# One more slab of the first projection computed among the modulation tiles, and the mixer tasks behind it dealt out anew

## The chip, the cores and the metric

The kernel runs on one core of a Trainium2 chip. The metric is device time in microseconds (us) for one execution; lower is better. Everything is float32, or float32 in the form that TensorE reads as fp32r.

## What is computed

The reference is a stack of four transformer-like layers over 256 tokens of width 2048. The part that matters here is the beginning of the first layer:

```python
c_act = jax.nn.silu(c)
mod = c_act @ w_ada[l] + b_ada[l]                       # 6 pieces of 2048
shift_a, scale_a, gate_a, shift_m, scale_m, gate_m = split(mod, 6)
h = rms_norm(x, g_pre_mix[l]) * (1.0 + scale_a) + shift_a
y = token_mixer(h, w_in[l], ...)                        # projection, conv, mLSTM, attention, w_out
x = x + gate_a * rms_norm(y, g_post_mix[l])
```

`token_mixer` multiplies h with `w_in` (2048 x 4616) and feeds the parts to a causal convolution, to an mLSTM with four heads and to a sliding-window attention with 16 heads.

## The kernel before

**Slabs.** Every weight matrix is cut into slabs of 2048 x 128 (1 MB, 16 blocks of 128 x 128). A slab gives 128 output features for all 256 tokens. The sequence of all slabs is numbered through the whole kernel; `w_in` of layer 0 has slabs 0 to 36, and `SLABS` says what each is: 0 `ka`, 1 `gate`, 2 `va`, 3 `qa0`, 4 `q0`, 5 `k0`, 6 `qa1`, 7 `v0`, 8 `v1`, 9 `qa2`, 10 `q1`, 11 `k1`, 12 `qa3`, and so on.

**An ordinary slab** takes three engines. It lands in one of five raw buffers (`RAW`, `RING` = 5). ScalarE copies it to `WH` in fp32r (`high`), VectorE subtracts that from the raw slab and writes the remainder `WL` (`low`), and TensorE (`slab`) multiplies 32 times with WH (the high and the low half of h, `HX`) and 16 times with WL. There are two places for WH and WL, taken in turn.

**The ramp.** The modulation is computed on VectorE: 16 tiles of `w_ada` for each of 12 pieces, each tile 1 MB, one `scalar_tensor_tensor` with a row sum (`tile`). The first two pieces, scale and shift, 32 tiles, have to be there before h is. They come in pairs, and after certain pairs (`RAMP_STEPS`) VectorE finishes the elements of scale and shift that are there (`ended`), forms x * scale * rms for those blocks of h (`scaled`, into `HF`), and ScalarE adds the shift. The first `RAMP` = 8 slabs of `w_in` are not split: they are loaded among the tiles (`RAMP_AT` gives the place in the order of loads, `RAMPW` the buffers) and multiplied in plain float32 with HF, block by block, as h comes (`ramp`). Each of the eight has a PSUM bank of its own (`BANK_OF`). `h_chunk_low` makes the low half of HX, four blocks at a time; three of the four chunks are made between tiles.

**Behind the ramp** each engine walks the slabs n = 8 to 36 of layer 0 in program order. At each slab ScalarE takes the result of slab n-1 out of PSUM, makes WH of slab n+1 and then does its mixer tasks; VectorE convolves if slab n-1 was q or k, computes the tiles that stand behind slab n (`AFTER`: further pieces of the modulation), makes WL of slab n+1 and then does its mixer tasks; TensorE multiplies slab n and then does its mixer tasks. Slabs 18, 21, 24, 27 and 30 are again computed in plain float32 from the raw buffer (`unsplit`). A mixer task i is whatever belongs behind slab i: `scores`, `turned` and `values` of an attention group, `m_scores`, `m_values`, `m_sum` of an mLSTM head, `gates`. In layer 0 the tasks 0 to 17 lag behind, because eight slabs were computed at once: `tasks_at` deals them to slabs 8 to 17 by hand.

**Waits that matter.** TensorE's `m_scores` of head 0, in task 8, waits for `s_grl`, which VectorE raises after it has split the gate rows `GRR`. VectorE's `attsums` in a task waits for ScalarE's `att_exp`, and that for VectorE's `att_max`. `m_divisor` waits through ScalarE for TensorE's `m_values`. All loads stand in one queue on SyncE: a load into a raw buffer waits until the load five places before it has been used up (`s_free`). Line 436 is the helper for all products, 440 for transposes, 949 for all of ScalarE's work; 1649 and 1657 are VectorE's `tensor_tensor` and `scalar_tensor_tensor`, 2648 a load into a raw buffer, 2699 a load of a ramp slab.

Of the kernel before, what the change touches and what calls it, by code (L numbers as in the profile page):

```python
# [13 lines left out]
T = 256  # L14
KT = 16
# [30 lines left out]

def tasks_at(l, n):

    late = {8: range(5), 9: (5,), 10: (6, 7), 11: (8,), 12: (9,), 13: (10, 11), 14: (12,), 15: (13, 14), 16: (15,),
            17: (16, 17)}  # L50
    return (n,) if l or n > 17 else late.get(n, ())


N_IN, N_LAYER = 37, 37 + 16 + 128
# [23 lines left out]

XN_AT = {2: 1, 3: 2, 4: 5, 5: 6}

RAMP = 8
RAMP_AT = [2, 6, 9, 13, 17, 21, 24, 28]
WIDE = {0, 1, 2, 5, 6, 7, 10, 11, 12}
RAMP_STEPS = [slice(_a, _b) for _a, _b in zip((0, 4, 8, 10, 12, 13, 14, 15), (4, 8, 10, 12, 13, 14, 15, 16))]


def spread(first, last, n):
# [1 line left out]

AFTER = ([9, 10, 11, 12, 13, 14, 15, 15, 16, 16, 17, 18, 19, 19, 20, 21, 22, 22, 23, 24, 25, 25, 26, 27, 28, 29, 30, 31,
          31, 32, 33, 33, 34, 35] + list(range(37, 51)) + spread(J_MLP[0] + 4, J_MLP[0] + 110, 82)
         + [J_IN[1] + n for n in (6, 7, 10, 15, 16, 18, 19, 24, 25, 29, 30, 31, 32, 33)]
         + [J_MLP[1] + n for n in (4, 6, 8)] + spread(J_MLP[1] + 19, J_MLP[1] + 31, 13))
# [54 lines left out]
    FREE_AT.append(_n)  # L150


BANK_OF = [j if 3 <= j < RAMP else (j + RAMP * (j < 3)) % 3 for j in range(N_SLABS)]

HI_AT, _n = [], 0
for _j in range(N_SLABS):
# [20 lines left out]

def before(j, of):

    return max([i for i in range(max(0, j - 8), j) if of[i] == of[j]], default=-1)  # L180


class Tally:
# [12 lines left out]
def build(nc, d, out):  # L196
    ctx = ExitStack()
    with ctx:
# [45 lines left out]
        CTANH = at("ctanh", (D,), A0)  # L244
        RAMPW = [m(f"rampw{r}", (KT, 128), off) for r, off in enumerate((12, 20, 28, 0, 52, 60, 68))]
        RAMPW.append(at("rampw7", (KT, 128), WL_AT + 8 * kb * PLACE_OF[RAMP + 1]))
        HF = m("hf", (KT, T), 36)
        SQ = m("sq", (KT, T + 1), 60)
        SQT = SQ[:, :, 0:T]
# [109 lines left out]
        s_a, s_v = sem("s_a"), sem("s_v")  # L359
        s_one, s_c, s_ct0, s_cb0 = sem("s_one"), sem("s_c"), sem("s_ct0"), sem("s_cb0")  # L360
        s_crow = sem("s_crow")
        s_rampw = [sem(f"s_rampw{r}") for r in range(RAMP)]
        s_hf = sem("s_hf")
        s_xs, s_xsum, s_rx = sem("s_xs"), sem("s_xsum"), sem("s_rx")
        s_ysq, s_yg, s_y2 = sem("s_ysq"), sem("s_yg"), sem("s_y2")
# [60 lines left out]
        def tensor(e):  # L426
# [58 lines left out]
            def ramp():  # L485


                banks = [claim(BANK_OF[r]) for r in range(RAMP)]

                def part(r, k):  # L490
                    return mm(banks[r][:, 0:T], RAMPW[r][:, k, :], HF[:, k, :], k == 0, k == KT - 1)

                here = []
                for q in RAMP_STEPS:
                    for r in range(len(here), RAMP):
                        if RAMP_AT[r] < 2 * q.stop:
                            here.append(r)
                            e.wait_ge(s_rampw[r], 16)
                            for k in range(q.start):
                                part(r, k)  # L500
                    for r in here:
                        for k in range(q.start, q.stop):
                            e.wait_ge(s_hf, k + 1)
                            last = part(r, k)
                        if q.stop == KT:
                            last.then_inc(s_slab, 1)
                for r in range(3, RAMP):
                    release[r] = (s_ev, r + 1)

            def side(i):  # L510

# [155 lines left out]
            def mixer_after(l, n):  # L667
                for i in range(8):
                    a = AT_SLAB["qa", i]
                    if n == a + 6:  # L670
                        turned(l, i)
                    if n == a + 7:
                        values(l, i)
                    if n == a + 1:
                        scores(l, i)
                if n == AT_SLAB["qa", 7] + 9:
                    att_sum(l)
                for i, s in enumerate(SLABS):
                    if s in V_ORDER and n == i + 1:
                        v_turned(l, i, TV[V_ORDER[s] % 2])  # L680
                if n == AT_G + 5:
                    gates(l)
                for h in range(4):
                    if n == AT_S[h]:
                        m_scores(l, h)
                    if n == AT_V[h]:
                        m_values(l, h)
                    if n == AT_V[h] + 2:
                        m_sum(l, h)
# [255 lines left out]
        def scalar(e):  # L945
# [24 lines left out]

            def whole(j):

                e.wait_ge(s_slab, j + 1)
                if j - 1 not in BY_SCALAR:
                    e.wait_ge(s_ev, j)
                return BK[BANK_OF[j]][:, 0:T]

            def log_and_exp():

# [12 lines left out]
                act(SX[:, :], BK[3][:, 0:T], ACT.Copy)  # L992
                rsqrt(RS[:, :], BK[3][:, 0:T], D, LN0[:, :], s_rx)

            def to_h_first(c, shift):

                q = slice(4 * c, 4 * c + 4)
                for k in range(4 * c, 4 * c + 4):
                    e.wait_ge(s_hs, k + 1)
                    act(HF[:, k, :], HF[:, k, :], ACT.Identity, bias=shift[:, k:k + 1]).then_inc(s_hf, 1)  # L1000
                e.wait_ge(s_hf, 4 * c + 4)
                act(HX[:, q, 0, :], HF[:, q, :], ACT.Copy).then_inc(s_hh, 1)

# [369 lines left out]
            def layer(l):  # L1373
                for n in range(0 if l else RAMP, N_IN):
                    if l == 0 and n == RAMP:
                        for i in range(RAMP):
                            mixer_half(l, i)
                    elif n:
                        mixer_half(l, n - 1)
                    for i in tasks_at(l, n):  # L1380
                        mixer_first(l, i)
                    if l or n != N_IN - 1:
                        next_high(J_IN[l] + n)
                    if l == 0 and n == N_IN - 2:
                        next_high(J_IN[l] + N_IN - 1)
                    if l and n == N_IN - 1:
                        out_gate(l, 5)
                    for i in tasks_at(l, n):
                        mixer_tasks(l, i)
                gate = modulation(l, GATE_A)  # L1390
                for n in range(16):
                    if n == 0:
# [235 lines left out]
            x_rms_first()  # L1628
            e.wait_ge(s_prm, 16)
            for c in range(4):  # L1630
                to_h_first(c, MOD[:, SHIFT_A, :])
            high(RAMP)
            layer(0)
            to_h(1, modulation(1, SHIFT_A))
# [5 lines left out]
        def vector(e):  # L1640
# [88 lines left out]
                e.wait_ge(s_mod, PIECES.index((l, piece)) - 1)  # L1729
                return MOD[:, 6 * l + piece, :]  # L1730

            def scaled(k, gs, first=False):
                stt((HF if first else SQT)[:, k, :], X[:, k, :], gs[:, k:k + 1], RS[:, :], ALU.mult,
                    ALU.mult).then_inc(s_hs, 1)

            def h_chunk_low(i, c):
# [309 lines left out]
            def mixer_tasks(l, n):  # L2046
                if n == AT_G + 4:
                    gates_scanned(l)
                if n == AT_G + 6:
                    e.wait_ge(s_gt, l + 1)  # L2050
                    e.tensor_copy(AC[:, :, :], BK[5][:, 0:8].rearrange("p (a h) -> p a h", a=2)).then_inc(s_ac, 1)
                    e.wait_ge(s_grh, l + 1)
                    tt(GRR[32:36, :, :], GR[0:4, :, :], GRR[0:4, :, :].bitcast(F32), ALU.subtract).then_inc(s_grl, 1)
# [540 lines left out]
                q = slice(512 * b, 512 * b + 512)  # L2594
                stt(CB[:, q], CTANH[:, q], 1.0, BK[4 + b][:, :], ALU.add, ALU.mult).then_inc(s_cb0, 1)
            e.wait_ge(s_cb0, 4)
            gs, sh = MOD[:, SCALE_A, :], MOD[:, SHIFT_A, :]
            for k in range(KT):
                tile(k)
                tile(16 + k)  # L2600
                if k % 4 == 0 and k:
                    h_chunk_low(-1, k // 4 - 1)
                for q in RAMP_STEPS:
                    if k == q.stop - 1:
                        e.wait_ge(s_prm, 16)
                        e.wait_ge(s_free, FREE_AT[TILE_POS[16 + k]])
                        ended(0, q)
                        settled(ended(1, q))
                        if k == 3:
                            e.wait_ge(s_rx, 1)  # L2610
                        for i in range(q.start, q.stop):
                            scaled(i, gs, True)
            for l in range(2):
                s0 = PER_LAYER * l + SINK
                settled(ts(MINUS_SINKS[:, 16 * l:16 * l + 16], PRM[:, s0:s0 + 16], -1.0, None, ALU.mult))
# [21 lines left out]
        def sync(e):  # L2637
# [56 lines left out]
            for place, (kind, n) in enumerate(LOADS):  # L2694
                if place in RAMP_AT:
                    r = RAMP_AT.index(place)
                    if r == 3:
                        e.wait_ge(s_crow, 4)
                    e.dma_start(RAMPW[r][:, :, :].rearrange("p a b -> p (a b)"), source(r)).then_inc(s_rampw[r], 16)
                if kind == "slab":  # L2700
                    if n == J_GLU + 2:
                        e.wait_ge(s_yq, 14)
                    others(n)
                    load(place, source(n))
                elif kind == "out":
                    if n == 0:
                        e.wait_ge(s_cc, 128)
                    load(place, c_keep[n].rearrange("p e k n -> p (e k n)"))
                else:
                    (l, piece), k = PIECES[n // 16], n % 16  # L2710
                    load(place, d["w_ada"][l, piece, k])
                if place == 4:
                    e.dma_start(PRM[:, :], d["prm"]).then_inc(s_prm, 16)
                if place == POS[RAMP + 1]:
                    e.dma_start(CST[:, :], d["cst"]).then_inc(s_cst, 16)
# [154 lines left out]
```

## Time and profile before

| what | value |
|---|---|
| device time, median of 3 runs | 3144.55 us (3142.89 to 3145.53) |
| the profiled execution: span from first to last instruction | 3145.5 us |
| TensorE busy, mean granted clock | 3075.0 us (98% of the span), 0.992 |
| VectorE busy | 2404.3 us (76%) |
| ScalarE busy | 1529.5 us (49%) |
| moved by DMA | 791.05 MB, mean 251 GB/s |

No time of the profiled execution other than its span is given; it lies 0.95 us above the median and within the three runs. The span is used as the base, and the difference is taken off at the end. A change here acts at the beginning of the kernel, so the table's shares say little: what counts is what each engine does between 80 and 230 us.

### The profile page before, as it was taken

Reading aid. Unit: us, or ns where it says so; the run is one execution under the profiler, and the core shown is the slowest. Engines: PE = TensorE matmul, PEld = TensorE weight load, DVE = VectorE, ACT = ScalarE, POOL = GpSimd, SP = SyncE. Lnnn points to the kernel's source line nnn. Section 1 sums busy time; section 2 is a strip of 40 time slices with the busy share of each in tenths; the row PEclk is TensorE's granted clock in tenths of the full one; section 3 lists DMA queues with packets and bytes.
Section 4 is the critical chain, followed back from the end, with each engine's and each line's share of the span. In section 5 each row is a group of like instructions: output and inputs, shape, how many; then the busy total and the mean of one; then the engine's idle time right before and its main releaser. Section 6 shows DMA issues by size and latency. Waiting matters only on the chain.

```text
span 3145.5 us, 61783 instructions
## 1 busy us (share of the span) xinstructions
PE 3075.0 (98%) x26577; PEld 2931.5 (93%) x26577; DVE 2404.3 (76%) x2964; ACT 1529.5 (49%) x2232; POOL 0.2 (0%) x4
## 2 busy tenths in 40 slices
PE   5999999999999999999999999999999999999999
PEld 3889999999999988989999999999899999999998
DVE  7898999788888788776887666687688767556764
ACT  2465664343434556666534444445433556434454
POOL 0000000000000000000000000000000000000000
PEclk7999999999999999999999999999999999999999
DMA  9888869999999745665688666895555554654453
GB/s 409 337 301 331 318 254 349 346 334 350 337 339 342 254 163 212 218 225 175 231 298 307 221 223 240 283 303 202 217 181 189 215 190 158 213 179 159 148 188 121
DMA packets 137025, 791.05 MB, mean 251 GB/s; under 512 B 20081, under 2 KB 38641, under 8 KB 46001
## 3 DMA queue, kind: packets, MB, share of 16 engines
q1 hardware_dynamic: 119714, 769.33, 67.2%
q10 hardware_dynamic: 17040, 17.76, 1.6%
q8 instruction: 211, 3.46, 0.4%
q14 instruction: 60, 0.49, 0.0%
HBM read 769.28 MB, written 17.76 MB: 250 GB/s over the span
## 4 chain that ended last, share of the span: by engine, by line
PE 53%; DVE 2%; ACT 1%; issue 0%; ACTq 0%; DVEq 0%
PE bk L436 52%; DVE wl L1649 1%; PE bk L440 0%; ACT wh L949 0%; DVE pr L1649 0%; DVE Hst L1649 0%; DVE xl L1649 0%; DVE ss L1649 0%; DVE qa L1657 0%; DVE p L1649 0%; DVE X L1649 0%; DVE raw L1657 0%; ACT ln L949 0%; DVE hg L1657 0%; ACT rsy L949 0%
## 5 line engine op out<-in xcount | busy, mean ns | idle before, releaser
L1649 DVE TENSOR_TENSOR wl<-raw,wh 128x2048 fp32r<-128x2048 f32 (+1 forms) x481 | 1092.5, 2271 | 321.1 <-ACT wh L949 318.1
L436 PE MATMUL bk<-HX,wh 128*128 128x256 f32 (+1 forms) x8058 | 1105.8, 294 | 1.8 <-ACT wh L949 1.6
L949 ACT ACTIVATE wh<-raw 128x2048 fp32r<-128x2048 f32 x477 | 911.8, 1912 | 351.1 <-PE bk L436 322.7
L436 PEld LDWEIGHTS bk<-HX,wh 128*128 128x128 f32 x8058 | 1022.2, 188 | 53.4 <-ACT wh L949 2.4
L436 PE MATMUL bk<-HX,wl 128*128 128x256 f32 x4560 | 569.0, 277 | 5.2 <-DVE wl L1649 5.2
L436 PEld LDWEIGHTS bk<-HX,wl 128*128 128x128 f32 x4560 | 542.3, 188 | 7.1 <-DVE wl L1649 7.0
L436 PE MATMUL bk<-hb,wh 128*128 128x256 f32 (+1 forms) x3916 | 488.0, 282 | 0.1
L436 PEld LDWEIGHTS bk<-hb,wh 128*128 128x128 f32 x3916 | 468.2, 188 | 8.2 <-issue 0.3
L1657 DVE SCALAR_TENSOR_TENSOR raw<-raw,cb 128x2048 f32<-128x2048 f32 x192 | 437.5, 2283 | 14.8 <-DMA raw<-in_w_ada 14.7
L436 PE MATMUL bk<-hb,wl 128*128 128x256 f32 x2048 | 253.8, 276 | 0.0
L436 PEld LDWEIGHTS bk<-hb,wl 128*128 128x128 f32 x2048 | 242.5, 188 | 0.0
L949 ACT ACTIVATE ur<-bk 128x256 f32<-128x256 f32 x122 | 46.8, 383 | 354.5 <-PE bk L436 338.4
L436 PE MATMUL bk<-sq,raw 128*128 128x257 f32 (+1 forms) x544 | 119.3, 379 | 0.0
L436 PEld LDWEIGHTS bk<-sq,raw 128*128 128x128 f32 x544 | 102.7, 189 | 17.4 <-issue 1.7
L949 ACT ACTIVATE yt<-bk 128x256 f32<-128x256 f32 x81 | 31.0, 383 | 164.8 <-PE bk L436 157.1
L436 PE MATMUL bk<-hf,rampw 128*128 128x256 f32 x256 | 65.6, 423 | 34.3 <-ACT hf L949 28.8
L436 PEld LDWEIGHTS bk<-hf,rampw 128*128 128x128 f32 x256 | 54.5, 215 | 45.4 <-issue 17.3
L1657 DVE SCALAR_TENSOR_TENSOR ur<-ur 128x256 f32<-128x256 f32 x122 | 51.6, 423 | 45.1 <-ACT ur L949 43.8
L1649 DVE TENSOR_TENSOR tacc<-tacc,ts 128x768 f32<-128x768 f32 (+1 forms) x84 | 72.5, 863 | 2.6 <-ACT yu L949 1.9
L436 PE MATMUL bk<-mx,wh 128*128 128x256 f32 (+1 forms) x483 | 64.8, 285 | 2.2 <-DVE mx L1649 2.1
L436 PE MATMUL bk<-ax,wh 128*128 128x256 f32 (+1 forms) x460 | 65.6, 294 | 0.1
L436 PEld LDWEIGHTS bk<-mx,wh 128*128 128x128 f32 x483 | 60.8, 188 | 4.7 <-ACT mx L949 2.1
(313 smaller groups left out, 2584.1 us busy)
## 6 DMA issues: line engine op xcount, KB each, us to landing
raw<-in_w_ada SPq DMA_DIRECT2D x192, 1024.0 KB, 6.9
raw<-in_w_up SPq DMA_DIRECT2D x128, 1024.0 KB, 6.5
raw<-in_w_down SPq DMA_DIRECT2D x128, 1024.0 KB, 5.7
raw<-in_w_in SPq DMA_DIRECT2D x66, 1024.0 KB, 5.3
raw<-in_kv_w SPq DMA_DIRECT2D x33, 1024.0 KB, 4.9
raw<-in_w_out SPq DMA_DIRECT2D x32, 1024.0 KB, 5.4
raw<-in_s_w_in SPq DMA_DIRECT2D x32, 1024.0 KB, 4.9
raw<-in_fox_w_in SPq DMA_DIRECT2D x32, 1024.0 KB, 4.8
```

The source lines that it names most:

```text
L436: return e.matmul(o_, l_, r_, start=start, stop=stop, skip_group_check=True)
L949: return e.activation(o_, i_, f, **kw)
L1649: return e.tensor_tensor(o_, a_, b_, op)
L1657: return e.scalar_tensor_tensor(o_, a_, s_, b_, op0, op1, accum_out=sums)
```

## The change

The ramp takes nine slabs instead of eight. Their loads stand earlier among the tiles. The ninth (slab 8) is summed in the second half of bank 7, beside the eighth, without a start flag of its own; its weights lie in the WH place of slab 10. VectorE no longer multiplies by scale: x * rms is formed once for all blocks, in four instructions after the second pair of tiles, and ScalarE's one instruction for each block applies scale and shift. The low halves of HX, chunks 0 to 2, are made after the last tile. The steps of the ramp become finer at the start (two blocks instead of four). The tasks 0 to 20 are dealt to the slabs 9 to 20; `gates` and the splitting of GRR come one task later in layer 0. Of the tiles behind the slabs, those of slabs 9 and 10 move to slab 18, which then has three.

```diff
-    late = {8: range(5), 9: (5,), 10: (6, 7), 11: (8,), 12: (9,), 13: (10, 11), 14: (12,), 15: (13, 14), 16: (15,),
-            17: (16, 17)}
-    return (n,) if l or n > 17 else late.get(n, ())
+    late = {9: range(5), 10: (5, 6), 11: (7,), 12: (8,), 13: (9,), 14: (10,), 15: (11, 12), 16: (13,), 17: (14, 15),
+            18: (16,), 19: (17, 18), 20: (19, 20)}
+    return (n,) if l or n > 20 else late.get(n, ())
...
-RAMP = 8
-RAMP_AT = [2, 6, 9, 13, 17, 21, 24, 28]
+RAMP = 9
+RAMP_AT = [2, 4, 7, 9, 12, 14, 17, 19, 22]
-RAMP_STEPS = [... zip((0, 4, 8, 10, 12, 13, 14, 15), (4, 8, 10, 12, 13, 14, 15, 16))]
+RAMP_STEPS = [... zip((0, 2, 4, 6, 8, 10, 12, 13, 14, 15), (2, 4, 6, 8, 10, 12, 13, 14, 15, 16))]
-AFTER = ([9, 10, 11, 12, 13, 14, 15, 15, 16, 16, 17, 18, 19, 19, 20, 21, ...
+AFTER = ([11, 12, 13, 14, 15, 15, 16, 16, 17, 18, 18, 18, 19, 19, 20, 21, ...
-BANK_OF = [j if 3 <= j < RAMP else (j + RAMP * (j < 3)) % 3 for j in range(N_SLABS)]
+BANK_OF = [7 if j == 8 else j if 3 <= j < RAMP else (j + RAMP * (j < 3)) % 3 for j in range(N_SLABS)]
+        RAMPW.append(at("rampw8", (KT, 128), WL_AT + 8 * kb * PLACE_OF[RAMP + 1] - 16 * kb))
...   TensorE, ramp
-                banks = [claim(BANK_OF[r]) for r in range(RAMP)]
+                banks = [claim(BANK_OF[r])[:, 0:T] for r in range(8)] + [BK[7][:, T:2 * T]]
-                    return mm(banks[r][:, 0:T], RAMPW[r][:, k, :], HF[:, k, :], k == 0, k == KT - 1)
+                    return mm(banks[r], RAMPW[r][:, k, :], HF[:, k, :], k == 0 and r < 8, k == KT - 1)
-                if n == AT_G + 5:
+                if n == AT_G + 5 + (l == 0):
                     gates(l)
...   ScalarE
-                    act(HF[:, k, :], HF[:, k, :], ACT.Identity, bias=shift[:, k:k + 1]).then_inc(s_hf, 1)
+                    act(HF[:, k, :], HF[:, k, :], ACT.Identity, scale=gs[:, k:k + 1],
+                        bias=shift[:, k:k + 1]).then_inc(s_hf, 1)
-                        for i in range(RAMP):
+                        for i in range(RAMP - 1):
                             mixer_half(l, i)
+                        e.wait_ge(s_slab, RAMP)
+                    if l == 0 and n == RAMP:
+                        mixer_half(l, RAMP - 1)
...   VectorE
-                if n == AT_G + 6:
+                if n == AT_G + 6 + (l == 0):
                     e.wait_ge(s_gt, l + 1)
-                if k % 4 == 0 and k:
-                    h_chunk_low(-1, k // 4 - 1)
+                if k == 1:
+                    e.wait_ge(s_rx, 1)
+                    for c in range(4):
+                        q = slice(4 * c, 4 * c + 4)
+                        tt(HF[:, q, :], X[:, q, :], bc(RS[:, :], 4), ALU.mult)
...
-                        settled(ended(1, q))
-                        if k == 3:
-                            e.wait_ge(s_rx, 1)
-                        for i in range(q.start, q.stop):
-                            scaled(i, gs, True)
+                        ended(1, q).then_inc(s_hs, q.stop - q.start)
+            for c in range(3):
+                h_chunk_low(-1, c)
...   SyncE
+                    if r == 8:
+                        e.wait_ge(s_rampw[0], 16)
```

## Rows read from the trace of the kernel before

**Rows 1.** The page, busy time by engine.

```profile
span 3145.5 us, 61783 instructions
PE 3075.0 (98%) x26577; PEld 2931.5 (93%) x26577; DVE 2404.3 (76%) x2964; ACT 1529.5 (49%) x2232; POOL 0.2 (0%) x4
```

**Rows 2.** Windows: length, busy (instructions) PE, PEld, DVE, ACT, POOL; clock, DMA share, GB/s.

```profile
90.00:94.00 4.00, 4.00 (x11) 3.19 (x10) 3.82 (x3) 0.31 (x1) 0.00 (x0) 0.50 1.01 420
...
110.00:114.00 4.00, 4.00 (x21) 3.51 (x20) 3.72 (x10) 0.33 (x1) 0.00 (x0) 1.00 1.02 421
...
166.00:170.00 4.00, 4.00 (x16) 3.47 (x17) 3.93 (x9) 0.31 (x2) 0.00 (x0) 0.57 0.94 352
...
121.00:150.00 29.00, 29.00 (x244) 28.22 (x243) 27.63 (x46) 20.90 (x38) 0.00 (x0) 1.00 0.61 225
150.00:223.00 73.00, 68.36 (x521) 62.92 (x521) 66.21 (x105) 42.14 (x108) 0.00 (x0) 0.98 0.81 302
223.00:330.00 107.00, 107.00 (x786) 100.56 (x785) 89.64 (x119) 64.12 (x130) 0.00 (x0) 1.00 0.85 335
```

**Rows 3.** VectorE in order of time, end of the ramp: start, us, instruction, idle before.

```profile
94.61 1.22 DVE L1649 TENSOR_TENSOR HX<-hf,HX 128x1024 fp32r<-128x1024 f32 x1
95.75 0.15 DVE L1649 TENSOR_TENSOR mod<-mod,prm 128x1 f32<-128x1 f32 x1
...
104.82 2.29 DVE L1657 SCALAR_TENSOR_TENSOR raw<-raw,cb 128x2048 f32<-128x2048 f32 x1 [0.19 <-DMA raw<-in_w_ada]
...
110.29 2.29 DVE L1657 SCALAR_TENSOR_TENSOR raw<-raw,cb 128x2048 f32<-128x2048 f32 x1
...
113.15 0.49 DVE L1657 SCALAR_TENSOR_TENSOR hf<-X,mod,rs 128x256 f32<-128x256 f32 x1
...
118.75 0.47 DVE L1653 TENSOR_SCALAR gi<-bk,prm 4x256 f32<-4x256 f32 x1 [2.16 <-PE bk L436]
...
119.64 2.27 DVE L1649 TENSOR_TENSOR wl<-raw,wh 128x2048 fp32r<-128x2048 f32 x1
...
125.90 2.28 DVE L1649 TENSOR_TENSOR wl<-raw,wh 128x2048 fp32r<-128x2048 f32 x1
```

**Rows 4.** TensorE in order of time, from the ramp to slab 21.

```profile
88.88 32.37 PE L436 MATMUL bk<-hf,rampw 128*128 128x256 f32 x136 [3.51 <-ACT hf L949]
...
127.91 4.04 PE L436 MATMUL bk<-HX,wh 128*128 128x256 f32 x32
...
133.67 3.93 PE L436 MATMUL bk<-HX,wh 128*128 128x256 f32 x32
...
146.37 0.49 PE L436 MATMUL bk<-grr,pk 128*128 128x512 f32 x1
...
160.22 2.15 PE L436 MATMUL bk<-HX,wl 128*128 128x256 f32 x16 [1.36 <-DVE wl L1649]
...
165.88 2.69 PE L436 MATMUL bk<-e,vm 128*128 128x256 f32 x8 [1.85 <-DVE e L1657]
...
219.66 2.04 PE L436 MATMUL bk<-HX,wl 128*128 128x256 f32 x16
221.54 1.47 PE L436 MATMUL bk<-e,vm 128*128 128x256 f32 x8
...
223.50 7.07 PE L436 MATMUL bk<-hf,raw 128*128 128x256 f32 x32
```

**Rows 5.** VectorE in order of time, between the ramp and slab 20.

```profile
143.25 0.68 DVE L1649 TENSOR_TENSOR grr<-gr,grr 4x512 fp32r<-4x512 f32 x1
...
203.69 0.36 DVE L1654 TENSOR_SCALAR sm<-sm 128x2 f32<-128x2 f32 x2
203.95 2.28 DVE L1649 TENSOR_TENSOR wl<-raw,wh 128x2048 fp32r<-128x2048 f32 x1
```

**Rows 6.** ScalarE and the load queue: a table load and a wait for a slab.

```profile
137.03 1.28 ACT L949 ACT_TABLE_LOAD   x1
...
211.55 1.92 ACT L949 ACTIVATE wh<-raw 128x2048 fp32r<-128x2048 f32 x1 [2.43 <-DMA raw<-in_w_in]
```

More of the change, by code:

```diff
@@ L79 @@
 XN_AT = {2: 1, 3: 2, 4: 5, 5: 6}
-RAMP = 8
-RAMP_AT = [2, 6, 9, 13, 17, 21, 24, 28]
+RAMP = 9
+RAMP_AT = [2, 4, 7, 9, 12, 14, 17, 19, 22]
 WIDE = {0, 1, 2, 5, 6, 7, 10, 11, 12}
-RAMP_STEPS = [slice(_a, _b) for _a, _b in zip((0, 4, 8, 10, 12, 13, 14, 15), (4, 8, 10, 12, 13, 14, 15, 16))]
+RAMP_STEPS = [slice(_a, _b) for _a, _b in zip((0, 2, 4, 6, 8, 10, 12, 13, 14, 15), (2, 4, 6, 8, 10, 12, 13, 14, 15, 16))]
 def spread(first, last, n):
     return [first + (last - first) * i // (n - 1) for i in range(n)]
-AFTER = ([9, 10, 11, 12, 13, 14, 15, 15, 16, 16, 17, 18, 19, 19, 20, 21, 22, 22, 23, 24, 25, 25, 26, 27, 28, 29, 30, 31,
+AFTER = ([11, 12, 13, 14, 15, 15, 16, 16, 17, 18, 18, 18, 19, 19, 20, 21, 22, 22, 23, 24, 25, 25, 26, 27, 28, 29, 30, 31,
           31, 32, 33, 33, 34, 35] + list(range(37, 51)) + spread(J_MLP[0] + 4, J_MLP[0] + 110, 82)
@@ L178, in before @@
 def before(j, of):
-    return max([i for i in range(max(0, j - 8), j) if of[i] == of[j]], default=-1)
+    return max([i for i in range(max(0, j - 9), j) if of[i] == of[j]], default=-1)
 class Tally:
@@ L361, in build @@
         s_crow = sem("s_crow")
-        s_rampw = [sem(f"s_rampw{r}") for r in range(RAMP)]
+        s_rampw = [sem(f"s_rampw{r}") for r in range(8)]
         s_hf = sem("s_hf")
@@ L497, in ramp @@
                             here.append(r)
-                            e.wait_ge(s_rampw[r], 16)
+                            e.wait_ge(s_rampw[r % 8], 16 * (r // 8 + 1))
                             for k in range(q.start):
@@ L506, in ramp @@
                             last.then_inc(s_slab, 1)
-                for r in range(3, RAMP):
+                for r in range(3, 8):
                     release[r] = (s_ev, r + 1)
+                release[7] = (s_ev, 9)
             def side(i):
@@ L971, in whole @@
             def whole(j):
-                e.wait_ge(s_slab, j + 1)
+                e.wait_ge(s_slab, j + 2 if j == 7 else j + 1)
                 if j - 1 not in BY_SCALAR:
                     e.wait_ge(s_ev, j)
-                return BK[BANK_OF[j]][:, 0:T]
+                return BK[BANK_OF[j]][:, T:2 * T] if j == 8 else BK[BANK_OF[j]][:, 0:T]
             def log_and_exp():
@@ L993, in x_rms_first, with to_h_first @@
                 rsqrt(RS[:, :], BK[3][:, 0:T], D, LN0[:, :], s_rx)
-            def to_h_first(c, shift):
+            def to_h_first(c, gs, shift):
                 q = slice(4 * c, 4 * c + 4)
@@ L1630, in scalar @@
             for c in range(4):
-                to_h_first(c, MOD[:, SHIFT_A, :])
+                to_h_first(c, MOD[:, SCALE_A, :], MOD[:, SHIFT_A, :])
             high(RAMP)
@@ L1730, in modulation, with scaled @@
                 return MOD[:, 6 * l + piece, :]
-            def scaled(k, gs, first=False):
-                stt((HF if first else SQT)[:, k, :], X[:, k, :], gs[:, k:k + 1], RS[:, :], ALU.mult,
+            def scaled(k, gs):
+                stt(SQT[:, k, :], X[:, k, :], gs[:, k:k + 1], RS[:, :], ALU.mult,
                     ALU.mult).then_inc(s_hs, 1)
@@ L2596, in vector @@
             e.wait_ge(s_cb0, 4)
-            gs, sh = MOD[:, SCALE_A, :], MOD[:, SHIFT_A, :]
             for k in range(KT):
@@ L2698, in sync @@
                         e.wait_ge(s_crow, 4)
-                    e.dma_start(RAMPW[r][:, :, :].rearrange("p a b -> p (a b)"), source(r)).then_inc(s_rampw[r], 16)
+                    if r == 8:
+                        e.wait_ge(s_rampw[0], 16)
+                    e.dma_start(RAMPW[r][:, :, :].rearrange("p a b -> p (a b)"), source(r)).then_inc(s_rampw[r % 8], 16)
                 if kind == "slab":
```

## The prediction

> **What bounds the kernel now.** I read the page first: TensorE is busy for 98% of the span [rows 1], so a slab that leaves its sequence could be worth its full time. But this change acts on 140 of 3145 us, so I went on to windows. Until 121 us the loads run at 421 GB/s with a DMA share of 1: the ramp is bound by DMA, and TensorE has gaps in it [rows 2, 4]. From 121 to 150 TensorE is fully busy, and VectorE is as good as full (27.6 of 29 us). From 150 to 223 TensorE idles 4.6 us and VectorE is busy for 66.2 of 73. From 223 to 330 TensorE has no gap and VectorE is busy for 89.6 of 107, so it has room again [rows 2]. Then I put the engines side by side in order of time. The waits of TensorE between 150 and 223 go to VectorE's results: 1.36 us for a WL, 1.85 us for an mLSTM product [rows 4]. So behind the ramp there is a stretch of 100 us with two engines near their limit, and VectorE is the one that TensorE waits for. The question is what the change does to VectorE there.
>
> **The loads.** 1 MB takes 2.49 us at 421 GB/s. The tile that VectorE began at 104.82 had just landed [rows 3]; it is the third from last, so the last was on hand at 104.82 + 2 x 2.49 = 109.8. With slab 8 loaded ahead it comes at 112.3. The later slabs' loads do not move: their bytes stand behind the same total. VectorE then needs 2.2 us for the tile and about 0.5 for `ended` (three small instructions; from the end of the tile to `scaled` in before, 112.50 to 113.15, with its wait 0.65): shift and scale of the last block at 115.1. Before, h's last product came at 113.15 + 0.49 = 113.6 [rows 3]. ScalarE adds 0.5: HF is complete at 115.7 instead of 114.2.
>
> **The ramp's end.** One product of the ramp is 7.07 / 16, about 0.43 us (last row of [rows 4], the same form). The last step is 9 of them, 3.9 us: end at 119.6, if TensorE has nothing left over. Before, it had: one slab came so late that its 15 blocks were made up at the end, and 68 products ran without a gap from 88.88 to 121.2 [rows 4]. With all nine slabs there by about 87 this is gone. I take 120.0, against 120.9 before; both ends, 119.6 and 121.5, change nothing below.
>
> **The slab removed.** An ordinary slab is 133.67 - 127.91 = 5.8 us of TensorE [rows 4], and 2.2 of VectorE. So TensorE alone is 5.8 + 0.9 = 6.7 us ahead.
>
> **VectorE.** `scaled` (16 x 0.45 or so) goes and four large products come (about 4.6 us, from the 1.22 of a chunk [rows 3]); both lie in DMA's shadow, and I cost them at nothing (without that cover they would be 7.2 less 4.6, a gain). The chunks of HX are another matter: three of 1.14 us (94.61 to 95.75 [rows 3]) leave that shadow and stand behind the last tile, in series. VectorE: 115.1 + 3.4 + 0.5 (sinks) + 1.2 (last chunk) = 120.2, then `gate_taken`, 0.9: 121.1. Before, it idled 2.16 us ahead of `gate_taken` and had that and WL of slab 8 behind it at 119.64 + 2.2 = 121.86 [rows 3]. So VectorE is ahead by 0.7 us only, where TensorE is ahead by 6.7.
>
> **The new order, slabs 9 to 12.** TensorE's `m_scores` of head 0 comes after four slabs behind the ramp, as before. By then VectorE must have split GRR. Before, it did that at 143.25 to 143.93 and TensorE came at 146.37 [rows 4, 5]. Between 119.64 and 143.93 VectorE had no idle time: 24.3 us for four WLs, two tiles, two convolutions, the scans, the first `att_max` and small things. Now GRR's split stands in task 8, dealt to slab 12, and there VectorE has by program order five WLs, two tiles and four convolutions ahead of it. A WL is 2.2 us and a convolution (125.90 - 119.64 - 2.2) / 2 = 2.0 [rows 3]: 24.3 + 2.2 (one WL more) + 4.1 (two convolutions more) = 30.6, so not before 151.7. Two waits come on top. Tasks 5 and 6 stand together on slab 10, so that `att_sums` directly follows `att_max` and waits for ScalarE's table load (1.28 [rows 6]) and exponentials, 1.9 us; and the convolution of k1 waits 0.5 for ScalarE's copy. That gives 154.5. TensorE: 120.2 + 4 x 5.8 + 2.5 of small products = 145.9 without waits; slab 12 waits 2.2 us for its WH, which stands on ScalarE behind those exponentials, and 0.7 for its WL: 148.8. It then stands still until 154.5: **a wait of 5.7 us that before does not have**. Its bounds are 2.9 (151.7 less 148.8, no waits on VectorE) and 8.6 (no waits on TensorE). With the two waits before it that is 8.6 us, more than the slab is worth.
>
> **The clock.** After a gap of 3.51 us TensorE ran at 0.50 in 90 to 94, and after 1.36 and 1.85 us near each other at 0.57 in 166 to 170 [rows 2, 4]. The products at 165.88 took 2.69 us, and the same ones later, at 221.54, 1.47 [rows 4]. The first case cost 32.4 - 68 x 0.43 = 3.2 us, the second some 1.7 with the sums behind. A gap of 5.7 should cost about 2.8. The Trainium skill ("TensorE: Matmul & The Clock Gate", "HAM oscillation") says that each long enough idle gap throttles the array anew and that the price is paid every time; the trace agrees for the gaps above.
>
> **Slabs 13 to 20.** Slab 13 starts at 155.4 (154.85 before, with 1.0 us of transposes already done) and ends at 164.0 with the clock's loss, against 162.3. Then before loses 1.85 and 1.7 at `m_values`, which it won't now: its data are early. Near slab 18 (start 200.8 before, with 2 us of products done that now come later) TensorE would be at 196.8: 2 us ahead. But `m_values` of head 0 and `m_divisor` now stand on one slab (15), and VectorE waits there through ScalarE for TensorE, which is late: some 7 us of idleness in all for slabs 13 to 15, where it has two tiles to do. Slab 18 then has a WL and three tiles, 19 two tiles and a WL, ahead of the `att_max` that before was done at 203.95 [rows 5]. That is 87 us of VectorE work from 121.1 (before it was 203.95 - 119.64 = 84.3, less about 6 of idle time [rows 2, 3, 5]; three tiles and a WL more make 8.8): 208 with no idle time, and 222.8 with the waits as I follow them. ScalarE's copy of `turned`, TensorE's `values` of the fourth group, `scores` and `m_values` stand behind it. Also, the load of slab 20 now waits for a tile at 208 instead of a WL at 206.2, and lands 5.3 us later (206.2 to 211.55 in before [rows 6]). Slab 21, which started at 223.50 [rows 4], starts at 229.6 with the clock's loss in full, and at 226.8 without it. Behind it VectorE has room [rows 2], PE's start carries to the end, and nothing is given back.
>
> **Sum.** Between +3.3 and +6.1 us; I take +5: 3145.5 + 5 = 3150.5, less 0.95 (how the profiled span stands to the median): 3149.5.
>
> **The rivals.** *The gain is kept.* VectorE's waits are filled, and TensorE arrives at slab 21 earlier. For: 208 with no idle time would allow 5.8 + 0.9 + up to 4 of the waits of before, 3144.5 - 5.8 to - 10: 3134 to 3139. Against: VectorE's 0.7 us. It decides if GRR is split before 147. *A draw.* The wait at `m_scores` comes, but without the clock's fall, or VectorE has half the idle time I follow: the slab's 5.8 against 5.7, 3141 to 3147.5. *It grows.* At slab 20 TensorE waits twice for about 3.8 us (the transposes of v3, then `values`), and the clock falls again: +2.8 on 6.1, and a late WL at slab 23: 3152 to 3157. The rule of the Trainium skill named above ("TensorE: Matmul & The Clock Gate"), taken literally, gives this one. *The ramp ends late*, if its products run at 0.50 through to step (8, 10): 124 instead of 120; it adds 3 us through WH of slab 11, and goes with the one before. That the ramp does not change is excluded.
>
> **How the numbers follow.** The forecast, 3147.5 to 3152, has 0.42; the draw 0.23; the kept gain 0.15; growth, the late ramp with it, 0.20. A difference under 0.2% (6.3 us: 3138.3 to 3150.8) is about what a measurement of this kernel can't tell from none. Faster than that: 0.15. Slower: growth and a third of the forecast, 0.35. Within: 0.50. The range, 3139 to 3156, leaves out most of the kept gain and the far end of growth.
>
> **What would show it.** The product with `grr` starts near 154.5 with over 4 us of idleness ahead of it; before it, two shorter waits at slab 12. The granted clock is at half in the 4 us behind. VectorE's `gi` is at 120.2 with no wait. Slab 21 (the second plain one of 16 products) starts later than 223.5. The prediction is wrong if `grr` is on time, if VectorE is through the chunks before 118, or if the time from slab 21 to the end changes by over 2 us.

## The result and the profile after

The changed kernel takes 3157.11 us (median of 4 runs, 3154.54 to 3158.48), the kernel before 3143.72 (4 runs, 3141.47 to 3145.53). The ratio is 1.0040 with a 95% interval of 1.0028 to 1.0053: **slower, by 9 to 17 us**. The forecast was slower by 5, the range ended at 3156.

First the page and the windows of the changed kernel, the latter with the columns of [rows 2].

```profile
span 3152.7 us, 61742 instructions
PE 3079.6 (98%) x26561; PEld 2933.6 (93%) x26561; DVE 2401.0 (76%) x2957; ACT 1529.9 (49%) x2231; POOL 0.2 (0%) x4
```

```profile
121.00:150.00 29.00, 25.94 (x202) 25.22 (x200) 25.42 (x44) 19.42 (x38) 0.00 (x0) 0.88 0.57 211
150.00:223.00 73.00, 58.18 (x424) 53.16 (x423) 60.67 (x88) 36.29 (x89) 0.00 (x0) 0.93 0.74 290
223.00:330.00 107.00, 107.00 (x767) 99.85 (x768) 89.11 (x127) 63.29 (x140) 0.00 (x0) 0.99 0.78 308
```

TensorE idles 3.1 us between 121 and 150, where [rows 2] has none, and 14.8 between 150 and 223 against 4.6. The unexpected column is VectorE's: it is *less* busy in both windows (25.4 and 60.7 against 27.6 and 66.2). Neither engine is full. They wait for each other. From 223 on TensorE is full again, as before.

TensorE in order of time, the rows that answer to [rows 4]; in brackets the idle time before an instruction and its releaser.

```profile
95.77 24.03 PE L437 MATMUL bk<-hf,rampw 128*128 128x256 f32 x108 [0.87 <-ACT hf L951]
119.44 3.98 PE L437 MATMUL bk<-HX,wh 128*128 128x256 f32 x32
...
141.94 6.43 PE L437 MATMUL bk<-HX,wh 128*128 128x256 f32 x32 [3.06 <-ACT wh L951]
...
153.82 0.44 PE L441 MATMUL bk<-cst,tv 128*128 128x128 f32 x2 [3.57 <-DVE ac L2057]
154.53 0.80 PE L437 MATMUL bk<-grr,pk 128*128 128x512 f32 x1 [0.27 <-DVE grr L1655]
...
197.44 0.85 PE L441 MATMUL bk<-cst,ta 128*128 128x128 f32 x6 [3.15 <-DVE sm L1660]
...
198.34 8.76 PE L437 MATMUL bk<-hf,raw 128*128 128x256 f32 x32
...
217.72 0.44 PE L441 MATMUL bk<-cst,tv 128*128 128x128 f32 x2 [3.12 <-ACT qa L951]
222.88 1.51 PE L441 MATMUL bk<-cst,ta 128*128 128x128 f32 x6 [4.71 <-DVE sm L1660]
...
224.47 4.62 PE L437 MATMUL bk<-HX,wh 128*128 128x256 f32 x32
228.93 2.05 PE L437 MATMUL bk<-HX,wl 128*128 128x256 f32 x16
230.90 0.87 PE L437 MATMUL bk<-ta,va 128*64 128x256 f32 x8
...
234.62 7.07 PE L437 MATMUL bk<-hf,raw 128*128 128x256 f32 x32
```

The ramp ends at 119.4, 1.5 us sooner than before. Then there are six waits, 17.9 us in sum. Slab 21, the last row, starts at 234.62 instead of 223.50. **The loss of 11.1 us is complete there.** The same lag, 11.4 us, is at the first norm of y: ScalarE's first `rsy` is at 434.9 before and at 446.3 after (first number after the durations).

```profile
L951 ACT ACTIVATE rsy<-ln x6: 416/417/418, 446.3 to 3141.6; 128x256 f32<-128x256 f32 x6
```

The last `rsy` comes only 7.2 us later than before's (3134.4). The difference of the medians is 13.4 us. The part behind the first `rsy` is the same in all kernels of this case, and it varies from execution to execution: from the first `rsy` to the last the twelve profiles have 2695.3 (the changed kernel) to 2702.4 us, and the one of before 2699.5. Also, in all runs that have both, time less span was 1.8 us, so the profiled span of before stands for about 3147.3 us, which is 3 to 4 above its median, and the profiled execution of the changed kernel was the fastest of its four. Below, the start of slab 21 in a profile is used beside the medians.

VectorE and ScalarE, in order of time.

```profile
114.87 3.49 DVE L1655 TENSOR_TENSOR HX<-hf,HX 128x1024 fp32r<-128x1024 f32 x3
...
119.83 0.47 DVE L1659 TENSOR_SCALAR gi<-bk,prm 4x256 f32<-4x256 f32 x1
...
153.80 0.68 DVE L1655 TENSOR_TENSOR grr<-gr,grr 4x512 fp32r<-4x512 f32 x1
...
222.37 0.36 DVE L1660 TENSOR_SCALAR sm<-sm 128x2 f32<-128x2 f32 x2
```

```profile
185.86 1.50 ACT L951 ACTIVATE ta<-ta,sm 128x256 f32<-128x256 f32 x4
...
203.19 1.50 ACT L951 ACTIVATE ta<-ta,sm 128x256 f32<-128x256 f32 x4
...
215.49 1.91 ACT L951 ACTIVATE wh<-raw 128x2048 fp32r<-128x2048 f32 x1 [7.96 <-DMA raw<-in_w_in]
217.31 0.37 ACT L951 ACTIVATE qa<-bk 128x256 f32<-128x256 f32 x1
...
225.17 0.85 ACT L951 ACTIVATE ta<-bk 128x384 f32<-128x384 f32 x2
```

GRR is split at 153.80, where [rows 5] have 143.25. WH of slab 20 starts at 215.49 after 8 us of idleness, against 211.55 after 2.4 [rows 6]. The first two rows of ScalarE are the last step on the attention weights of groups 2 and 3 before TensorE may transpose them; they are needed below.

The clock in short windows around four of the waits, with the columns of [rows 2]: the granted clock is the last but two.

```profile
141.00:145.00 4.00, 3.06 (x14) 3.06 (x15) 3.93 (x6) 2.58 (x6) 0.00 (x0) 0.50 0.00 0
...
153.00:157.00 4.00, 2.91 (x10) 2.40 (x11) 3.87 (x12) 0.66 (x2) 0.00 (x0) 0.64 0.94 383
...
197.00:201.00 4.00, 3.56 (x15) 3.04 (x16) 1.94 (x8) 3.67 (x14) 0.00 (x0) 0.69 0.11 43
...
222.00:226.00 4.00, 3.12 (x16) 3.15 (x17) 1.59 (x8) 3.23 (x14) 0.00 (x0) 0.53 1.02 426
```

Behind the ramp the clock fell to its lower level four times, where before it did once (166 to 170 in [rows 2]). Against the usual durations the products took longer by 6.43 - 4.04 = 2.4 us at slab 12; 1.6 at the product with grr and slab 13; 8.76 - 7.07 = 1.7 at slab 18; 1.5 at the transposes and slab 20: 7.2 in all. That is not yet a delay of slab 21. The 2.4 us at slab 12 stand ahead of a wait for VectorE, and without them TensorE would have waited 2.4 us longer there.

### The profile page after: what moved, and what is told of

It is laid out like the page before. It is cut to its first block, busy times and chain, and to the rows that moved or that the text cites. A ratio compares the mean times of both kernels' runs of the same rounds, so it can differ in the third digit from the quotient of the medians.

```text
span 3152.7 us, 61742 instructions
## 1 busy us (share of the span) xinstructions
PE 3079.6 (98%) x26561; PEld 2933.6 (93%) x26561; DVE 2401.0 (76%) x2957; ACT 1529.9 (49%) x2231; POOL 0.2 (0%) x4
## 4 chain that ended last, share of the span: by engine, by line
PE 53%; DVE 2%; ACT 1%; issue 0%; ACTq 0%; DVEq 0%
PE bk L437 52%; DVE wl L1655 1%; PE bk L441 0%; ACT wh L951 0%; DVE pr L1655 0%; DVE Hst L1655 0%; DVE xl L1655 0%; DVE ss L1655 0%; DVE qa L1663 0%; DVE p L1655 0%; DVE X L1655 0%; DVE raw L1663 0%; ACT ln L951 0%; DVE hg L1663 0%; ACT rsy L951 0%
## 5 line engine op out<-in xcount | busy, mean ns | idle before, releaser
L437 PE MATMUL bk<-hf,rampw 128*128 128x256 f32 x288 | 74.0, 422 | 23.6 <-ACT hf L951 22.3
```

Of the source, the lines that this page charges most:

```text
L437: return e.matmul(o_, l_, r_, start=start, stop=stop, skip_group_check=True)
```

## The experiments

Three theories. **A**: the new dealing puts a consumer on TensorE and its producer on VectorE or ScalarE on the same slab, and each such pair is a wait. **B**: VectorE's total work is the bound from the ramp to slab 21, and no single wait matters. **C**: the three low chunks, now in series behind the last tile, are the cost. The first four kernels are the changed one with one thing altered.

**Gates back to their tasks.**

```diff
-                if n == AT_G + 5 + (l == 0):      # TensorE
+                if n == AT_G + 5:
-                if n == AT_G + 6 + (l == 0):      # VectorE
+                if n == AT_G + 6:
```

> The changed kernel with only the gate transposes and the splitting of GRR put back to tasks 6 and 7, as before. In the changed kernel TensorE waits 3.6 + 0.3 us at the product with grr and loses about 1.6 us more to the clock there. Theory A (the new dealing puts TensorE behind results that VectorE makes on the same slab): the product with grr has no wait, slab 13 starts about 4 us earlier, and slab 21 starts 2 to 5 us earlier than 234.6. Theory B (VectorE's total work between the ramp and slab 21 is the bound, the place of single waits is not): slab 13 starts earlier, but slab 21 within 1 us of 234.6.

Measured: 3152.99 us, ratio to before 1.0029 (1.0018 to 1.0041). TensorE:

```profile
135.62 0.25 PE L441 MATMUL bk<-cst,gi 4*128 4x4 f32 x2 [2.60 <-DVE gt L1655]
149.94 0.48 PE L437 MATMUL bk<-grr,pk 128*128 128x512 f32 x1
...
177.04 1.12 PE L441 MATMUL bk<-cst,ta 128*128 128x128 f32 x6 [2.99 <-DVE sm L1660]
...
230.44 7.07 PE L437 MATMUL bk<-hf,raw 128*128 128x256 f32 x32
```

The product with grr has no wait, and slab 21 comes 4.2 us sooner. B's number, under 1 us, is missed. A new wait of 2.6 us takes the place of one: the gate transposes now stand on slab 10, with the scans they need. The 2.99 us at 177.04 are new too. They stand at the transposes of group 1, which share slab 15 with the `att_max` of group 2; the changed kernel came there too late to wait. The wait of 3.15 us at group 2 is gone in return.

**The pairs of before, one slab later.**

```diff
-    ... 14: (10,), 15: (11, 12), 16: (13,), 17: (14, 15), 18: (16,), 19: (17, 18), 20: (19, 20)}
+    ... 14: (10, 11), 15: (12,), 16: (13, 14), 17: (15,), 18: (16, 17), 19: (18,), 20: (19, 20)}
```

> The changed kernel with tasks 10 to 18 dealt in the pairs of before, one slab later: 14: (10, 11), 15: (12), 16: (13, 14), 17: (15), 18: (16, 17), 19: (18). Then the att_max that frees banks 3 and 4 stands a slab ahead of the transposes that claim them, not on the same slab. Theory A: the waits of 3.15 and 4.7 us at the transposes of groups 2 and 3 go, and the half clock behind them (about 3 us); slab 21 starts 5 to 9 us earlier than 234.6. Theory B (VectorE's work is the bound): under 2 us.

Measured: 3147.60 us, ratio 1.0010 (1.0001 to 1.0019), **9.5 us less than the changed kernel** by the medians. TensorE:

```profile
141.97 5.56 PE L437 MATMUL bk<-HX,wh 128*128 128x256 f32 x32 [2.83 <-ACT wh L951]
...
153.85 0.69 PE L441 MATMUL bk<-cst,tv 128*128 128x128 f32 x2 [4.43 <-DVE ac L2057]
...
211.29 0.85 PE L441 MATMUL bk<-cst,ta 128*128 128x128 f32 x6 [0.97 <-DVE sm L1660]
214.15 0.44 PE L441 MATMUL bk<-cst,tv 128*128 128x128 f32 x2 [2.01 <-ACT vm L951]
225.41 7.07 PE L437 MATMUL bk<-hf,raw 128*128 128x256 f32 x32
```

The waits at 141.97 and 153.85 stay. The 3.15 at the transposes of group 2 is gone, that of group 3 is 0.97 instead of 4.71, and slab 21 comes 9.2 us sooner, just above A's 5 to 9. No work was taken off VectorE: B, with its number of under 2 us, is refuted for this stretch.

**Two tiles of slab 18 to slabs 27 and 29.**

```diff
-AFTER = ([... 17, 18, 18, 18, 19, 19, 20, ... 26, 27, 28, 29, 30, ...
+AFTER = ([... 17, 18, 19, 19, 20, ... 26, 27, 27, 28, 29, 29, 30, ...
```

> The changed kernel with two of the three tiles of slab 18 moved to slabs 27 and 29. ScalarE idles 8 us for slab 20's weights in the changed kernel, because their load waits behind a tile of slab 18. Theory A: VectorE is 4.4 us earlier at slab 20, the load comes about 2 us earlier, TensorE's waits of 3.1 and 4.7 us shrink to 4 or less in sum, slab 21 starts 3 to 6 us earlier. Theory B (VectorE's work is the bound): 4.4 us earlier, the two tiles, and TensorE has time to lose them at 27 and 29, so 4 us in the total as well. Against both: no change if the waits come from the order of tasks alone.

Measured: 3155.97 us, ratio 1.0036 (1.0023 to 1.0048), not told apart from the changed kernel. Slab 21 at 230.55, 4.1 us sooner, of which 2.7 are left at the first `rsy` (434.9 + 8.7). TensorE:

```profile
198.52 1.51 PE L441 MATMUL bk<-cst,ta 128*128 128x128 f32 x6 [3.12 <-DVE sm L1660]
...
220.18 0.85 PE L441 MATMUL bk<-cst,ta 128*128 128x128 f32 x6 [3.00 <-DVE sm L1660]
```

The wait for slab 20's load is gone, those at the two groups' transposes are not. The late load was a part, and not the main one. The gain at slab 21 lies in A's 3 to 6 us, and B named about the same, so this run does not part the two.

**The chunks between the tiles again.**

```diff
+                if k % 4 == 0 and k:
+                    h_chunk_low(-1, k // 4 - 1)
...
-            for c in range(3):
-                h_chunk_low(-1, c)
```

> The changed kernel with the three low chunks of HX made between the tiles again, as before. Theory A: VectorE's gate_taken comes 2.3 to 3.4 us earlier, GRR is split 2 to 3 us earlier, but HF may be complete up to 1 us later; slab 21 starts 1 to 3 us earlier. Theory C (the chunks behind the last tile are the main cost of the change): slab 21 starts 5 us or more earlier, because each wait of TensorE for VectorE shrinks by 3.

Measured: 3157.74 us, ratio 1.0043 (1.0029 to 1.0057); slab 21 at 235.09. VectorE:

```profile
117.75 1.23 DVE L1655 TENSOR_TENSOR HX<-hf,HX 128x1024 fp32r<-128x1024 f32 x1 [1.53 <-ACT HX L951]
119.82 0.47 DVE L1659 TENSOR_SCALAR gi<-bk,prm 4x256 f32<-4x256 f32 x1 [0.85 <-ACT ka L951]
```

`gi` starts at 119.82, as in the changed kernel, and GRR is split at 153.76 against 153.80. VectorE now waits for ScalarE's HX and `ka` instead. The place of the three chunks costs nothing here: C is refuted, and the chunks are not why GRR is late. A's numbers for this run, GRR 2 to 3 us and slab 21 1 to 3 us earlier, are missed as well.

**The dealing alone, on the kernel before**, with its eight-slab ramp: `tasks_at`, the gates' `+ (l == 0)` and `AFTER` are taken from the change.

> The kernel before, with its eight-slab ramp, and of the change only the new dealing of tasks, the gates one task later and the new places of the tiles. Theory A (the dealing is what costs): slower than before by 5 to 14 us, with waits at the transposes of groups 2 and 3. Theory C (the nine-slab ramp with its chunks behind the last tile is what costs): within 2 us of before.

Measured: 3167.84 us, ratio 1.0068 (1.0056 to 1.0081), slower than before by 23 us by the medians, by 18 to 25 by the interval; A had 5 to 14. TensorE:

```profile
163.93 0.69 PE L440 MATMUL bk<-cst,tv 128*128 128x128 f32 x2 [4.17 <-DVE ac L2051]
...
208.45 0.85 PE L440 MATMUL bk<-cst,ta 128*128 128x128 f32 x6 [3.13 <-DVE sm L1654]
...
229.08 0.69 PE L440 MATMUL bk<-cst,tv 128*128 128x128 f32 x2 [5.15 <-ACT qa L949]
234.24 1.51 PE L440 MATMUL bk<-cst,ta 128*128 128x128 f32 x6 [4.46 <-DVE sm L1654]
```

These four waits are those of the changed kernel, 10 to 11 us later; slab 21 starts at 246.34. So with the eight-slab ramp the dealing costs 23 us, and the nine-slab ramp under the same dealing gives back 11 (3167.84 to 3157.11): the ramp is the good half of the change. The two figures hold for this order of adding them. The dealing was made for nine slabs, and what it costs with nine is not measured alone.

**Pairs and gates together**, the edits of the first two:

> The pairs of before and the gates at tasks 6 and 7, together; the nine-slab ramp stays. Slab 21 started at 225.4 with the pairs alone, and the gates alone brought 4.2 us. Theory A (each wait is a cost of its own, they add): slab 21 at 221 to 222, and at the first rms of y the kernel is 1 to 3 us ahead of before, total 3141 to 3144. Theory B (VectorE's total work is the bound by now): slab 21 at 224 or later, no better than the pairs alone.

Measured: 3144.98 us, ratio 1.0001 (0.9993 to 1.0010); slab 21 at 221.63. The single gains add (225.4 - 221.6 = 3.8, against 4.2 alone), as A says. The first `rsy` is 1.9 us ahead of before. The whole loss is gone; of A's 3141 to 3144 in the total the median shows nothing.

**And WH of slab 12 sooner**, on ScalarE:

```diff
-                    if l or n != N_IN - 1:
+                    if (l or n != N_IN - 1) and (l or n != 11):
                         next_high(J_IN[l] + n)
+                    if l == 0 and n == 10:
+                        next_high(J_IN[l] + 11)
```

> As the last, and ScalarE makes WH of slab 12 on slab 10, ahead of its gate rows and exponentials, where it idled 5.2 us. The wait of 2.8 us at slab 12 and its half clock (about 1.6) go. Theory A: slab 21 3 to 4 us earlier than in the last kernel, 217 to 219, total 3138 to 3141. Theory B: TensorE only reaches its next wait for VectorE sooner, under 1 us.

Measured: 3144.91 us, ratio 0.9998 (0.9989 to 1.0007); slab 21 at 223.00. Nothing gained, and both of A's numbers are missed. The wait that it was to remove had already gone in the kernel before it: the gate transposes' 2.6 us on slab 10 had taken its place.

**And two tiles later**, the edit of the third:

> As the last, and two of the three tiles of slab 18 at slabs 27 and 29. Theory A: the waits of 1.0 and 2.0 us for slab 20 go, 1 to 3 us. Theory B (VectorE's work is the bound): 4 us, the two tiles. If VectorE has no room at 27 and 29, it is given back at the end of the layer's projection.

Measured: 3143.69 us, ratio 0.9993 (0.9984 to 1.0002); slab 21 at 216.99, 6.5 us ahead of before, 4.6 at the first `rsy`. A miss upwards for slab 21 (6 us against 1 to 4); of the total, nothing that can be told from no change.

**Gate transposes behind slab 11, only GRR's split kept early:**

```diff
-                if n == AT_G + 5:                  # TensorE
+                if n == AT_G + 5 + (l == 0):
```

> As the last of the combined kernels (pairs of before, two tiles later, WH of slab 12 sooner), but TensorE's gate transposes go back to task 7, behind slab 11, and only VectorE's splitting of GRR stays at task 7. On slab 10 the transposes waited 2.6 us for the scans of the same slab. Theory A: that wait and the half clock behind it (about 1.5 us) go, slab 21 at 213 to 215 instead of 217.0, total 3138 to 3141, clearly faster than before. Theory B (VectorE is the bound between 120 and 160): the wait moves to WL of slab 13, slab 21 within 1 us of 217.0.

Measured: **3142.66 us, ratio 0.9990 (0.9981 to 0.9999)**; slab 21 at 217.12. TensorE:

```profile
146.77 3.78 PE L437 MATMUL bk<-HX,wl 128*128 128x256 f32 x16 [3.49 <-DVE wl L1657]
```

The 2.6 us are gone, and 3.49 us for the WL of slab 12 stand in their place. Here B holds, though it named the WL of the next slab: up to slab 13, VectorE sets the pace. Of the ten kernels this is the one whose interval lies below 1, by little, and one of ten may do so by chance; the expected 3138 to 3141 are not reached.

**The same, WH of slab 12 at its old place:**

> As the one before, with WH of slab 12 at its old place behind the exponentials. Both theories: the wait of 2.8 us for it at slab 12 is back. Theory A: slab 21 3 to 4 us later than there, with the half clock. Theory B: VectorE's time covers it, under 1 us.

Measured: 3142.42 us, ratio 0.9993 (0.9984 to 1.0002); slab 21 at 217.40. WH's wait of 2.83 us is back, WL's is 0.59 and not 3.49. The two waits cover one another: B again. The total cannot be told from that of the kernel before it.

## Why the prediction was half right

*Direction and place* were right: slower, with the loss made between the ramp and slab 21 and still there at the first norm (11.4 us). The rival of a kept gain did not come: TensorE was 7.3 us ahead on its own (5.8 for the slab, 1.5 for the ramp), and then stood still for results and banks that VectorE and ScalarE had not yet given. The size was wrong: +5 forecast, +13.4 measured, and 3157.11 lies above the range.

*Loads, end of the ramp, GRR.* The last shift and scale were forecast for 115.1 and came at 114.95; the ramp's end 120.0, measured 119.44; `gi` 120.2, measured 119.83; GRR's split ends at 154.5 in both. That last hit is in part luck: the terms written down, 121.1 + 30.6 + 1.9 + 0.5, give 154.1. The waits from slab 12 to the product with grr sum to 6.9 us, forecast 8.6, with 2.4 more in the half clock between, which hid in the same wait. The wait for the WL of slab 12 did not come, and ahead of grr there were 3.57 + 0.27 us of idleness where I had asked for over 4.

*The chunks* were wrong in their weight. They end late (118.69 + 1.22 = 119.91), but the first gate row needs ScalarE's `ka` at the same time, as the experiment with the chunks inside shows.

*"Slabs 13 to 20"* is the step that failed. I forecast that the `att_max` of group 4, on slab 19, would be done at 222.8, and it was done at 222.73. Behind it I put ScalarE's copy of `turned`, `values`, `scores` and `m_values`: 6.8 us, with no slab among them, and slab 21 at 229.6. So I had TensorE do the transposes of group 3 and the whole of slab 20 ahead of that `att_max`. It could not. The transposes write banks 3 and 4, which are free only after the `att_max` of the next group has read them, and the new dealing puts both on slab 19. They started at 222.88, slab 20 at 224.47, and `values`, for which ScalarE's copy was ready at 225.17 + 0.85 = 226.0, at 230.90. These 4.9 us are the 5.0 by which slab 21 was late against the forecast (234.62 less 229.6). About 1.5 of them are the clock behind the wait, the rest is the slab in the wrong place.

The transposes of group 2 and the `att_max` of group 3 share slab 17 in the same way: 3.15 us, which the forecast did not have. I followed the data that each product needs and not the bank that it writes. The order of the tasks did not change, only which of them share a slab. The experiment with the pairs of before took 3.7 us of the wait at group 3 and all of that at group 2.

That the bank is the reason, and not the data, can be read from the trace. `turned` waits for two things, its data and the bank. Its data were ready at 185.86 + 1.50 = 187.4 for group 2 and at 204.7 for group 3, 10 and 18 us before the transposes started. The releaser, `sm`, is the last instruction of the next group's `att_max`. Two more of the six waits are of this kind: the transposes `tv` at 153.82 and 217.72 claim bank 5, which VectorE's `ac` and ScalarE's `qa` had still to read on the same slab. No run gave the transposes a bank of their own, so what the banks alone cost is not measured.

*The clock*: one fall, 2.8 us, was forecast; four falls, 7.2 us of longer products, were measured. Not all of that reached slab 21. The 2.4 us at slab 12 did not, the last 1.5 did. The 3.3 between stand ahead of longer waits for VectorE, and reach slab 21 only as far as VectorE in turn waited for TensorE; no run separates that. The growth rival, 3152 to 3157, had two waits at slab 20 and a second fall of the clock there, as measured; its late WL at slab 23 did not come. The rule of the Trainium skill ("TensorE: Matmul & The Clock Gate", "HAM oscillation") that the price comes again at each long gap fitted this trace better than my single fall: the clock fell after 3.06, 3.57, 3.15 and 4.71 us of idleness. The rule is about long gaps, and I had called the short ones of before, 1.36 and 1.85 us, agreement; the last section shows that a short gap may or may not bring the clock down.

*The choice of +5* out of a range of 3.3 to 6.1 had no row that spoke for the lower half; the part with the clock in full was 6.1.

*The rest*, 11.4 us of lag at the first norm against 13.4 between the medians, is not explained. It is less than what the profiles differ by behind the first `rsy`. So the last sign that I named, the time from slab 21 to the end, was too sharp for one profile of each: it is 2922.0 us before and 2918.1 in the changed kernel, over 2 us apart, but the twelve profiles have 2918.1 to 2926.8. That nothing is given back there is neither shown nor refuted.

## What to carry to other kernels

When tasks are dealt out anew between in-order engines, check for each one not only where its data come from but also who frees the buffer it writes, and keep the two a slab apart: here the reader of a bank and the next writer of it. A gain of one engine in a stretch where it waits for another is worth only as much as the other is ahead. Split a change of this kind: here the ramp was good for 11 us and the dealing bad for 23. The old pairs and the earlier gates took back the whole loss of 13 us. With two tiles moved away and the gate transposes put back as well, the median was 2 us below before, which is at the edge of what these runs can tell.

## What the runs showed of the hardware

The same gap does not always cost the same. In the kernel with the pairs of before, TensorE waited 2.83 us for WH of slab 12, and in the last kernel also 2.83 us at the same place. Just behind the gap the windows read, with the columns of [rows 2]:

```profile
142.00:146.00 4.00, 4.00 (x24) 4.00 (x25) 4.00 (x4) 1.61 (x5) 0.00 (x0) 0.67 0.25 37
```

```profile
142.00:146.00 4.00, 3.39 (x28) 3.39 (x29) 3.96 (x5) 2.25 (x6) 0.00 (x0) 1.00 0.06 8
```

The granted clock is 0.67 in the first window and 1.00 in the second. In the first kernel the 32 products took 5.56 us, in the second 4.04. With the chunks inside, a gap of only 1.84 us there was followed by 5.51 us. So in these runs a gap of about 2 to 3 us cost 1.5 us on top or nothing. Part of the scatter between executions of one kernel may come from that; with one profile of each kernel this is not shown.
